# A fused hybrid layer on one Trainium2 core: the first two feed-forward units read the residual times the norm's weight, and the token factor goes onto their result tiles

## The chip, the cores and the metric

The kernel runs on one core of a Trainium2 chip. The metric is the device time of one execution in microseconds (us), as a median over runs.

## What is computed

Two blocks run one after the other on 512 tokens of width 1024, all in float32. The first mixes an RWKV-7 branch and a sparse attention branch. The second has three gated branches and then a feed-forward part with a short convolution. The change touches only the passage into that feed-forward part:

```python
def _rmsnorm(x, g):
    xf = x.astype(jnp.float32)
    r = lax.rsqrt(jnp.mean(xf * xf, axis=-1, keepdims=True) + EPS)
    return (xf * r).astype(x.dtype) * g
...
x = x + _mixer(...)                    # ends in merged @ w_o
h = _rmsnorm(x, norm_ffn_g)            # r: one factor per token, g: one weight per channel
u = _causal_dwconv(h @ w_up, conv_ffn_w)      # 3 taps along the tokens, 2 x 2816 channels
gt, up = jnp.split(u, 2, axis=-1)
x = x + (jax.nn.silu(gt) * up) @ w_down
```

Since r belongs to the token alone, (x * r * g) @ w_up equals ((x * g) @ w_up) * r.

## The kernel before, in words

**Layout.** Activations are stored with channels on the 128 partitions and the 512 tokens along the row: a tensor of width 1024 is 8 chunks of 128x512. Every product of two float32 numbers on TensorE is made from three passes over parts (`tile`, L402 to L404): high x high, low x high, high x low. So every operand is split into a rounded high part and a low part that holds the rest.

**Units.** All weights arrive in a fixed order in units of 8x128 rows by 256 columns (1 MB, `weight_units`). A unit gives two result tiles of 128x512, m = 0 and 1, each with 8 chunks k and three passes: 48 matmuls per unit. There are two weight buffers, taken in turn. For each unit u SyncE loads `w_raw` (`load`), ScalarE copies it into `w_hi` (`split_hi`, L1256), GpSimd takes the difference into `w_lo` (`split_lo`, L1204), and TensorE waits for both (`next_unit`). ScalarE may write the buffer of u only when TensorE is through with u-2 (`slot_used`). ScalarE does so where its own written order has a call of `after_unit()`, which splits the unit two ahead. Whatever stands in front of that call on ScalarE also delays the weights.

**Order within a unit.** `unit_tiles` without `ready` makes tile 0 and then tile 1. With `ready` it goes by chunks, both tiles for each chunk, and waits ahead of each chunk. Result tiles go round 8 PSUM banks in turn; a bank is used again when VectorE has counted it free.

**The passage.** Units "wo2" 0 to 3 (merged @ w_o) are added to the residual `x_res` by VectorE (`residual`, L2196), and ScalarE squares the new chunks (`sq_f`, L1670). VectorE adds the squares of chunks 0 to 5 together (`sum_squares`, L2208). TensorE then sums over the channels (`token_sums`, L384: 12 float32 matmuls of one column each, 24 records), VectorE makes the variance and its reciprocal (L2217, L2220), ScalarE the root (L1267), and TensorE spreads the 512 token factors over all partitions (`spread`, L393: 4 matmuls, 8 records). Only then does VectorE scale each chunk by weight and token factor (`scaled_chunk`, L1747), ScalarE rounds it (`hi_chunks`, L1302) and VectorE takes the low part (`lo_chunk`, L1758); unit "up" 0 starts on chunk 0 as soon as that is there.

**The up units.** There are 22 (`FC`). For unit i and each tile m, ScalarE writes the last convolution tap from the bank to `conv_f` (L1678), VectorE adds the two other taps from the bank (L2459) and frees the bank. ScalarE then calls `after_unit()` and makes the sigmoid (L1682); VectorE multiplies twice (L2465, L2467) and splits the result in parts for the down product (L1736, L1737), which counts `act_ready`. `conv_f` has two sets, so the taps of unit i wait until unit i-2 has counted `act_ready`. Every one of the three engines follows its own written order.

Of the kernel before, what the change touches and what calls it, by code (L numbers as in the profile page):

```python
# [16 lines left out]
F32 = mybir.dt.float32  # L17
F32R = mybir.dt.float32r
ALU = mybir.AluOpType
# [101 lines left out]
MASS_ORDER = [(odd, q) for q in range(NT) for odd in range(2)]  # L121
SCORE_AT = [(0, 0), (0, P), (1, 0), (2, 0)]
FIRST_POOL_UNIT = 9
MIX_ORDER = [*range(NI, CH), *range(NI)]


# [4 lines left out]
def build(nc, dram, out):  # L131
# [3 lines left out]
    with ctx:  # L135
        base = -(-nc.sbuf_base // 32) * 32

        def at(name, offset, shape, dt=F32):
            return nc.alloc_sbuf_tensor_at(name, [P] + shape, dt, offset=base + offset)
# [3 lines left out]
        def sem(name):  # L143
            if name not in sems:
                sems[name] = ctx.enter_context(nc.semaphore(name))
            return sems[name]
# [96 lines left out]
        merged_hi = at("merged_hi", R0 + 32768, [CH, T], F32R)  # L243
        merged_lo = at("merged_lo", R0 + 49152, [CH, T], F32R)
        sq_f = at("sq_f", R0, [CH, T])
        pad_a = at("pad_a", R0 + 73728, [KA - 1 + T])
        rs_mix = tmp[2][:, 0:T]
        u_sig = tmp[2][:, 0:T]
# [48 lines left out]
        def take(eng, key):  # L297

            b, n = seq[key]
            eng.wait_ge(full[b], n + 1)  # L300
            return ps[b]
# [5 lines left out]
        def evacuated(eng, key):  # L307

            b, n = seq[key]
            eng.wait_ge(free[b], n + 1)  # L310
# [24 lines left out]
        def _(pe):  # L335
# [39 lines left out]
            def token_sums(key, sq):  # L375

                b = bank(key)
                for n, c in enumerate((0, CH - 2, CH - 1)):
                    if n:
                        pe.wait_ge(sem("sq_" + key), c + 1)  # L380
                    else:
                        pe.wait_ge(sem("summed_" + key), 1)
                    for t in range(NT):
                        mm = nc.tensor.matmul(b[:, t:t + 1], sq[:, c, t * P:t * P + P], ones[:, 0:1], start=n == 0 and t == 0,  # L384
                                              stop=n == 2, skip_group_check=True)
                done(mm, key)

            def spread(key, col, b=None):

                if b is None:  # L390
                    b = bank(key)
                for t in range(NT):
                    mm = nc.tensor.matmul(b[:, t * P:t * P + P], col[:, t:t + 1].to_broadcast([P, P]), ident[:, :], start=True, stop=True)  # L393
                done(mm, key)
# [16 lines left out]
            def unit_tiles(what, i, xh, xl, width=T, tiles=2, ready=None, branch=None, order=range(CH), between=None):  # L411

                u = next_unit(what)
                keys = [(what, i, m) if branch is None else (what, branch, i, m) for m in range(tiles)]
                if ready is None:
                    for m in range(tiles):
                        b = bank(keys[m])
                        done(tile(b, u, m * P, width, xh, xl), keys[m])
                        if m == 0 and between is not None:
                            between()  # L420
                else:
                    bs = [bank(key) for key in keys]
                    for n, k in enumerate(order):
                        if callable(ready):
                            ready(k)
                        else:
                            pe.wait_ge(sem(ready), n + 1)
                        for m in range(tiles):
                            mm = tile(bs[m], u, m * P, width, xh, xl, start=n == 0, stop=n == CH - 1, ks=[k])
                            if n == CH - 1:  # L430
                                done(mm, keys[m])
                unit_last[u] = keys[-1]
# [641 lines left out]
            gated(1)  # L1074
            for i in range(4):
                unit_tiles("wo2", i, merged_hi, plain(merged_lo), ready=None if i else "merged_ready")
            token_sums("f", sq_f)
            pe.wait_ge(sem("tok_f_ready"), 1)
            spread("rs_f", tok_rs)
            for i in range(FC):  # L1080
                unit_tiles("up", i, oh, ol, ready=None if i else "ffn_ready")
            for i in range(4):
                bs = None
                for k0 in (0, 8, 16):
# [157 lines left out]
        def _(act):  # L1242
# [17 lines left out]
            def root(t=rs[:, :], done="rs_ready"):  # L1260

                if done == "rs_ready":
                    roots[0] += 1
                    act.wait_ge(sem("var_ready"), roots[0])
                else:
                    act.wait_ge(sem(done.replace("ready", "var")), 1)
                A(t, t, ACT.Sqrt).then_inc(sem(done), 1)  # L1267
# [30 lines left out]
            def hi_chunks(which, name):  # L1298

                for c in range(*which):  # L1300
                    act.wait_ge(sem(name + "_scaled"), c + 1)
                    A(op_hi[:, c, :], tmp[c % 2][:, 0:T], ACT.Copy).then_inc(sem(name + "_hi"), 1)  # L1302
# [228 lines left out]
            def after_unit():  # L1531

                nonlocal u
                split_hi(u + 2)
                u += 1
# [127 lines left out]
            for i in range(4):  # L1663
                filled(act, ("wo2", i, 1))
                after_unit()
                if i == 2:
                    A(misc[:, 127:128], ones[:, 0:1], ACT.Sqrt)
                for c in (2 * i, 2 * i + 1):
                    evacuated(act, ("wo2", i, c % 2))
                    A(sq_f[:, c, :], x_res[:, c, :], ACT.Square).then_inc(sem("sq_f"), 1)  # L1670
            root(tok_rs, "tok_f_ready")
            hi_chunks((0, CH), "ffn")
            for i in range(FC):
                for m in range(2):
                    if i >= 2:
                        act.wait_ge(sem("act_ready"), i - 1)

                    A(conv_f[i % 2][m][:, 0:T], take(act, ("up", i, m))[:, :], ACT.Copy,  # L1678
                      scale=pcol("conv_ffn_w_2", 4 * FC + FC * m + i)).then_inc(sem("tap_ready"), 1)
                after_unit()  # L1680
                evacuated(act, ("up", i, 0))
                A(sig_f[i % 2][:, 0:T], conv_f[i % 2][0][:, 0:T], ACT.Sigmoid).then_inc(sem("cg_sig"), 1)  # L1682
            for i in range(4):
# [14 lines left out]
        def _(dve):  # L1698
# [504 lines left out]
            def sum_squares(key, sq, i):  # L2203

                dve.wait_ge(sem("sq_" + key), 2 * i + 2)
                for c in (2 * i, 2 * i + 1):
                    if c:
                        ins = V.tensor_tensor(sq[:, 0, :], sq[:, 0, :], sq[:, c, :], ALU.add)  # L2208
                        if c == CH - 3:
                            ins.then_inc(sem("summed_" + key), 1)  # L2210
                        else:
                            link(ins)
# [220 lines left out]
            for c in range(CH):  # L2433
                parts(conv_b[:, c, :], op2_hi[:, c, :], op2_lo[:, c, :], "op2_ready1")
            gate_steps(1)
            for i in range(4):
                if i:
                    sum_squares("f", sq_f, i - 1)
                residual("wo2", i)
            for i in range(4):  # L2440
                for m in range(2):
                    evacuated(dve, ("wo2", i, m))
            token_variance("f", 1.0 / D, EPS2).then_inc(sem("tok_f_var"), 1)
            r_f = take(dve, "rs_f")
            for c in range(CH):
                scaled_chunk("norm_ffn_g_2", c, r_f, "ffn")
                if c:
                    lo_chunk(c - 1, "ffn")
# [4 lines left out]
            for i in range(FC):  # L2453
                for m in range(2):
                    b, y = take(dve, ("up", i, m)), conv_f[i % 2][m]
                    dve.wait_ge(sem("tap_ready"), 2 * i + m + 1)
                    for back in (1, 2):
                        w = pcol("conv_ffn_w_2", 2 * FC * (2 - back) + FC * m + i)
                        ins = V.scalar_tensor_tensor(y[:, back:T], b[:, 0:T - back], w, y[:, back:T], ALU.mult, ALU.add)  # L2459
                        if back == 1:  # L2460
                            link(ins)
                    evac(ins, ("up", i, m))
                g, y = sig_f[i % 2][:, 0:T], conv_f[i % 2]
                dve.wait_ge(sem("cg_sig"), i + 1)
                link(V.tensor_tensor(g, g, y[0][:, 0:T], ALU.mult))  # L2465
                evacuated(dve, ("up", i, 1))
                link(V.tensor_tensor(g, g, y[1][:, 0:T], ALU.mult))  # L2467
                lo = act_lo[:, i, :] if i < 16 else act_lo2[:, i - 16, :]
                parts(g, act_hi[:, i, :], lo, "act_ready")
# [73 lines left out]
```

## Time and profile before

| what | value |
|---|---|
| median of 3 runs | 1470.88 us (1470.73 to 1476.52) |
| the profiled execution, its own time | 1469.24 us |
| its span in the trace | 1467.4 us (1.84 us lie around it) |
| mean granted TensorE clock | 0.982 |
| TensorE matmuls busy | 1408.8 us, 96% of the span |
| VectorE, ScalarE, GpSimd busy | 64%, 33%, 33% |
| DMA | 125.14 MB, mean 85 GB/s |

A time in the trace is counted from the start of the span. "PE" is TensorE, "PEld" its weight loads, "DVE" VectorE, "ACT" ScalarE, "POOL" GpSimd. `L402` is a line of the kernel. A matmul of 512 columns is shown with its full length of about 0.39 us, while the next starts 0.23 us after it, so the distance between starts is what counts. "<-" in brackets names what an engine was waiting for. The granted clock is 1.00 at 2.4 GHz and 0.50 at 1.2 GHz.

### The profile page before, as it was taken

The page shows a single profiled execution, that of the slowest core. Times are in us where ns is not written, and L with a number is a line of the kernel's source. Part 1 is how long each engine was busy: PE and PEld are TensorE (multiplying, and loading weights), DVE is VectorE, ACT ScalarE, POOL GpSimd, SP SyncE. Part 2 cuts the span into 40 slices and gives each one's busy share as a digit, 9 for nine tenths or more (in the row PEclk, how much of TensorE's full clock was granted, in tenths as well). Part 3 has the DMA queues.
Part 4 walks back from the last instruction along what each step waited for, and adds up shares of the span by engine and source line. Part 5 has one row for each costly group of instructions (what it writes and reads, how often), then busy time and mean ns, then how long its engine had stood idle before and what let it go on. Part 6 is the DMA issues. An engine that isn't in the chain of part 4 may idle for free.

```text
span 1467.4 us, 18610 instructions
## 1 busy us (share of the span) xinstructions
PE 1408.8 (96%) x7612; PEld 1144.1 (78%) x7612; DVE 933.8 (64%) x1322; ACT 487.7 (33%) x663; POOL 487.6 (33%) x131
## 2 busy tenths in 40 slices
PE   7999978699998999999999999999989999999997
PEld 6778646587888877888888887878878888888886
DVE  6679868735413357769969974762457888885122
ACT  5443367243324232122222223322233333332121
POOL 0004110012535323343434433334423443443441
PEclk9999999799999999999999999999989999999999
DMA  6221000023314211232232231222222223222221
GB/s 206 87 87 58 29 2 2 4 85 118 129 71 144 87 58 58 86 100 102 86 105 97 87 115 58 86 98 104 86 87 86 87 88 113 87 99 95 84 96 58
DMA packets 21349, 125.14 MB, mean 85 GB/s; under 512 B 2384, under 2 KB 3408, under 8 KB 7696
## 3 DMA queue, kind: packets, MB, share of 16 engines
q1 hardware_dynamic: 20752, 121.71, 23.6%
q10 hardware_dynamic: 512, 2.23, 0.4%
q8 instruction: 61, 1.00, 0.3%
q14 instruction: 24, 0.20, 0.0%
HBM read 121.84 MB, written 2.10 MB: 84 GB/s over the span
## 4 chain that ended last, share of the span: by engine, by line
PE 88%; DVE 8%; ACT 3%; issue 1%; DMA 0%; DVEq 0%; SPq 0%; ACTq 0%
PE bank L402 25%; PE bank L404 24%; PE bank L403 24%; PE bank L1008 1%; PE bank L1024 1%; PE bank L354 1%; DVE conv_b L2406 1%; PE bank L393 1%; ACT prob L1409 1%; PE bank L877 1%; PE bank L958 1%; PE bank L626 0%; ACT probT L1415 0%; PE bank L362 0%; DVE op_hi L1736 0%
## 5 line engine op out<-in xcount | busy, mean ns | idle before, releaser
L1204 POOL TENSOR_TENSOR w_lo<-w_raw,w_hi 128x2048 fp32r<-128x2048 f32 (+1 forms) x102 | 468.2, 4590 | 762.8 <-ACT w_hi L1256 746.9
L402 PE MATMUL bank<-op_hi,w_hi 128*128 128x512 f32 x1344 | 529.8, 394 | 6.4 <-DVE op_lo L1758 2.3
L404 PE MATMUL bank<-op_hi,w_lo 128*128 128x512 f32 x1344 | 525.9, 391 | 0.0
L403 PE MATMUL bank<-op_lo,w_hi 128*128 128x512 f32 x1344 | 525.9, 391 | 0.0
L402 PEld LDWEIGHTS bank<-op_hi,w_hi 128*128 128x128 f32 x1344 | 253.6, 189 | 63.7 <-issue 6.3
L404 PEld LDWEIGHTS bank<-op_hi,w_lo 128*128 128x128 f32 x1344 | 253.3, 188 | 54.6
L403 PEld LDWEIGHTS bank<-op_lo,w_hi 128*128 128x128 f32 x1344 | 253.4, 189 | 54.0 <-issue 0.7
L1256 ACT ACTIVATE w_hi<-w_raw 128x2048 fp32r<-128x2048 f32 (+2 forms) x109 | 205.6, 1887 | 265.3 <-PE bank L404 265.3
L2299 DVE SCALAR_TENSOR_TENSOR bank<-pad_b,par,bank 128x512 f32<-128x512 f32 x232 | 175.3, 756 | 7.8
L2465 DVE TENSOR_TENSOR tmp<-tmp,conv_f 128x512 f32<-128x512 f32 x22 | 101.6, 4617 | 16.4 <-ACT tmp L1682 16.4
L2196 DVE TENSOR_TENSOR x_res<-bank,x_res 128x512 f32<-128x512 f32 x24 | 16.5, 691 | 136.9 <-PE bank L404 136.8
L402 PE MATMUL bank<-act_hi,w_hi 128*128 128x512 f32 x176 | 69.4, 394 | 0.0
L404 PE MATMUL bank<-act_hi,w_lo 128*128 128x512 f32 x176 | 69.3, 394 | 0.0
L403 PE MATMUL bank<-act_lo,w_hi 128*128 128x512 f32 x176 | 69.2, 393 | 0.0
L1678 ACT ACTIVATE conv_f<-bank,par 128x512 f32<-128x512 f32 x33 | 22.7, 689 | 101.6 <-PE bank L404 101.6
L2459 DVE SCALAR_TENSOR_TENSOR conv_f<-bank,par,conv_f 128x511 f32<-128x511 f32 x66 | 49.2, 747 | 10.9 <-ACT conv_f L1678 9.7
L2380 DVE TENSOR_TENSOR tmp<-bank,gate 128x512 f32<-128x512 f32 x16 | 11.1, 692 | 57.8 <-PE bank L404 57.7
L1605 ACT ACTIVATE gate<-bank,par 128x512 f32<-128x512 f32 x24 | 16.4, 688 | 79.6 <-PE bank L404 79.6
L404 PEld LDWEIGHTS bank<-act_hi,w_lo 128*128 128x128 f32 x176 | 33.1, 188 | 7.8
L403 PEld LDWEIGHTS bank<-act_lo,w_hi 128*128 128x128 f32 x176 | 33.1, 188 | 7.7
L402 PEld LDWEIGHTS bank<-act_hi,w_hi 128*128 128x128 f32 x176 | 33.1, 188 | 7.6
L1195 POOL TENSOR_SCALAR_AFFINE_SELECT score<-score 128x128 f32<-128x128 f32 x3 | 0.9, 295 | 90.7 <-DVE misc L1896 90.7
(374 smaller groups left out, 1702.0 us busy)
## 6 DMA issues: line engine op xcount, KB each, us to landing
w_raw<-in_w_units SPq DMA_DIRECT2D x104, 1024.0 KB, 4.9
w_raw<-in_w_units SPq DMA_DIRECT2D x4, 768.0 KB, 4.2
x_res<-in_x SPq DMA_DIRECT2D x8, 256.0 KB, 6.5
x_res<-in_x ACTq DMA_DIRECT2D x2, 1024.0 KB, 6.3
out<-x_res SPq DMA_DIRECT2D x8, 256.0 KB, 2.2
w_raw<-in_w_units SPq DMA_DIRECT2D x3, 512.0 KB, 9.0
w_raw<-in_w_units SPq DMA_DIRECT2D x4, 256.0 KB, 5.6
mem_tok<-in_mem SPq DMA_DIRECT2D x1, 1024.0 KB, 5.2
```

What stands on the lines that cost most here:

```text
L354: mm = nc.tensor.transpose(b[:, j * P:j * P + rows], src, ident[0:rows, 0:rows])
L402: nc.tensor.matmul(b[:, 0:width], h, xh[:, x0 + k, 0:width], start=start and k == ks[0], stop=False)
L403: nc.tensor.matmul(b[:, 0:width], h, xl(x0 + k, width), start=False, stop=False)
L404: mm = nc.tensor.matmul(b[:, 0:width], l, xh[:, x0 + k, 0:width], start=False, stop=stop and k == ks[-1])
L1204: nc.gpsimd.tensor_tensor(w_lo[u % 2][:, 0:nk, :], w_raw[u % 2][:, 0:nk, :], w_hi[u % 2][:, 0:nk, :].bitcast(F32), ALU.subtract).then_inc( ...
L1256: A(w_hi[u % 2][:, 0:nk, 0:n], w_raw[u % 2][:, 0:nk, 0:n], ACT.Copy).then_inc(hi_ready, 1)
L1605: evac(A(gates[m][:, :], take(act, ("pg", branch, i, m))[:, :], ACT.Sigmoid, bias=pcol("b_gate_2", 8 * branch + 2 * i + m)), ("pg", branch ...
L1678: A(conv_f[i % 2][m][:, 0:T], take(act, ("up", i, m))[:, :], ACT.Copy, scale=pcol("conv_ffn_w_2", 4 * FC + FC * m + i)).then_inc(sem("tap_ ...
L2196: evac(V.tensor_tensor(x, b[:, :], x, ALU.add), (what, i, m))
L2299: ins = V.scalar_tensor_tensor(to, pad[:, k:k + T], pcol("conv_b_w_2", 8 * k + i), y, ALU.mult, ALU.add)
L2459: ins = V.scalar_tensor_tensor(y[:, back:T], b[:, 0:T - back], w, y[:, back:T], ALU.mult, ALU.add)
L2465: link(V.tensor_tensor(g, g, y[0][:, 0:T], ALU.mult))
```

## The change

Three things are changed. VectorE and ScalarE make, for each residual chunk, the parts of x times the norm's weight (`plain_hi`, `plain_lo`), beside the squares. Units "up" 0 and 1 read these parts, with the token sums placed ahead of chunk 3 of unit 0 and the spread ahead of chunk 7; VectorE multiplies each of their four result tiles by the token factor, in the bank, before the taps. And ScalarE splits the weights of "up" 2 ahead of `hi_chunks` and those of "up" 3 behind it, both ahead of the taps of unit 0; the calls behind the taps stay from unit 2 on. From unit 2 on the normed parts are read as before, with the waits for their chunks in unit 2.

```diff
--- before.py
+++ after.py
@@ -121,6 +121,7 @@
 MASS_ORDER = [(odd, q) for q in range(NT) for odd in range(2)]
 SCORE_AT = [(0, 0), (0, P), (1, 0), (2, 0)]
 FIRST_POOL_UNIT = 9
+PLAIN_UNITS = 2
 MIX_ORDER = [*range(NI, CH), *range(NI)]
 
 
@@ -243,6 +244,8 @@
         merged_hi = at("merged_hi", R0 + 32768, [CH, T], F32R)
         merged_lo = at("merged_lo", R0 + 49152, [CH, T], F32R)
         sq_f = at("sq_f", R0, [CH, T])
+        plain_hi = at("plain_hi", R0 + 16384, [CH, T], F32R)
+        plain_lo = at("plain_lo", 65536, [CH, T], F32R)
         pad_a = at("pad_a", R0 + 73728, [KA - 1 + T])
         rs_mix = tmp[2][:, 0:T]
         u_sig = tmp[2][:, 0:T]
@@ -1074,11 +1077,20 @@
             gated(1)
             for i in range(4):
                 unit_tiles("wo2", i, merged_hi, plain(merged_lo), ready=None if i else "merged_ready")
-            token_sums("f", sq_f)
-            pe.wait_ge(sem("tok_f_ready"), 1)
-            spread("rs_f", tok_rs)
-            for i in range(FC):
-                unit_tiles("up", i, oh, ol, ready=None if i else "ffn_ready")
+
+            def statistics(k):
+                pe.wait_ge(sem("plain_ready"), k + 1)
+                if k == 3:
+                    token_sums("f", sq_f)
+                elif k == CH - 1:
+                    pe.wait_ge(sem("tok_f_ready"), 1)
+                    spread("rs_f", tok_rs)
+
+            unit_tiles("up", 0, plain_hi, plain(plain_lo), ready=statistics)
+            for i in range(1, PLAIN_UNITS):
+                unit_tiles("up", i, plain_hi, plain(plain_lo))
+            for i in range(PLAIN_UNITS, FC):
+                unit_tiles("up", i, oh, ol, ready=None if i > PLAIN_UNITS else "ffn_ready")
             for i in range(4):
                 bs = None
                 for k0 in (0, 8, 16):
@@ -1667,17 +1679,24 @@
                     A(misc[:, 127:128], ones[:, 0:1], ACT.Sqrt)
                 for c in (2 * i, 2 * i + 1):
                     evacuated(act, ("wo2", i, c % 2))
+                    A(plain_hi[:, c, :], x_res[:, c, :], ACT.Copy, scale=pcol("norm_ffn_g_2", c)).then_inc(sem("plain_hi"), 1)
                     A(sq_f[:, c, :], x_res[:, c, :], ACT.Square).then_inc(sem("sq_f"), 1)
             root(tok_rs, "tok_f_ready")
+            after_unit()
             hi_chunks((0, CH), "ffn")
+            for i in range(1, PLAIN_UNITS):
+                after_unit()
             for i in range(FC):
                 for m in range(2):
                     if i >= 2:
                         act.wait_ge(sem("act_ready"), i - 1)
+                    if i < PLAIN_UNITS:
+                        act.wait_ge(sem("up_scaled"), 2 * i + m + 1)
 
                     A(conv_f[i % 2][m][:, 0:T], take(act, ("up", i, m))[:, :], ACT.Copy,
                       scale=pcol("conv_ffn_w_2", 4 * FC + FC * m + i)).then_inc(sem("tap_ready"), 1)
-                after_unit()
+                if i >= PLAIN_UNITS:
+                    after_unit()
                 evacuated(act, ("up", i, 0))
                 A(sig_f[i % 2][:, 0:T], conv_f[i % 2][0][:, 0:T], ACT.Sigmoid).then_inc(sem("cg_sig"), 1)
             for i in range(4):
@@ -2433,15 +2452,24 @@
             for c in range(CH):
                 parts(conv_b[:, c, :], op2_hi[:, c, :], op2_lo[:, c, :], "op2_ready1")
             gate_steps(1)
+            def plain_parts(i):
+                for c in (2 * i, 2 * i + 1):
+                    dve.wait_ge(sem("plain_hi"), c + 1)
+                    V.scalar_tensor_tensor(plain_lo[:, c, :], x_res[:, c, :], pcol("norm_ffn_g_2", c), plain_hi[:, c, :].bitcast(F32),
+                                           ALU.mult, ALU.subtract).then_inc(sem("plain_ready"), 1)
+
             for i in range(4):
                 if i:
                     sum_squares("f", sq_f, i - 1)
+                    plain_parts(i - 1)
                 residual("wo2", i)
+            plain_parts(3)
             for i in range(4):
                 for m in range(2):
                     evacuated(dve, ("wo2", i, m))
             token_variance("f", 1.0 / D, EPS2).then_inc(sem("tok_f_var"), 1)
             r_f = take(dve, "rs_f")
+            link(V.tensor_copy(rs[:, :], r_f[:, :]))
             for c in range(CH):
                 scaled_chunk("norm_ffn_g_2", c, r_f, "ffn")
                 if c:
@@ -2453,6 +2481,8 @@
             for i in range(FC):
                 for m in range(2):
                     b, y = take(dve, ("up", i, m)), conv_f[i % 2][m]
+                    if i < PLAIN_UNITS:
+                        V.tensor_tensor(b[:, :], b[:, :], rs[:, :], ALU.mult).then_inc(sem("up_scaled"), 1)
                     dve.wait_ge(sem("tap_ready"), 2 * i + m + 1)
                     for back in (1, 2):
                         w = pcol("conv_ffn_w_2", 2 * FC * (2 - back) + FC * m + i)
```

## Rows read from the trace of the kernel before

**Rows 1.** page, part 1: engine, busy us (share), instructions
```profile
PE 1408.8 (96%) x7612; PEld 1144.1 (78%) x7612; DVE 933.8 (64%) x1322; ACT 487.7 (33%) x663; POOL 487.6 (33%) x131
```

**Rows 2.** page, part 4: the chain that ended last
```profile
PE 88%; DVE 8%; ACT 3%; issue 1%; DMA 0%; DVEq 0%; SPq 0%; ACTq 0%
```

**Rows 3.** timeline of TensorE, 1074 to 1100 us: start, length, instruction, idle before
```profile
1080.48 0.95 PE L384 MATMUL bank<-ones,sq_f 128*128 128x1 f32 x8
1083.24 2.44 PE L384 MATMUL bank<-ones,sq_f 128*128 128x1 f32 x16 [1.82 <-ACT sq_f L1670]
1086.49 2.08 PE L393 MATMUL bank<-ident,misc 128*128 128x128 f32 x8 [0.81 <-ACT misc L1267]
1090.89 0.77 PE L402 MATMUL bank<-op_hi,w_hi 128*128 128x512 f32 x1 [2.32 <-DVE op_lo L1758]
...
1094.44 0.56 PE L404 MATMUL bank<-op_hi,w_lo 128*128 128x512 f32 x1
```

**Rows 4.** timeline of ScalarE, 1032 to 1140 us
```profile
1047.16 1.92 ACT L1256 ACTIVATE w_hi<-w_raw 128x2048 fp32r<-128x2048 f32 x1 [9.28 <-PE bank L404]
...
1058.36 1.92 ACT L1256 ACTIVATE w_hi<-w_raw 128x2048 fp32r<-128x2048 f32 x1 [8.24 <-PE bank L404]
...
1080.76 1.91 ACT L1256 ACTIVATE w_hi<-w_raw 128x2048 fp32r<-128x2048 f32 x1 [6.72 <-PE bank L404]
1082.58 1.13 ACT L1670 ACTIVATE sq_f<-x_res 128x512 f32<-128x512 f32 x2
1086.23 0.21 ACT L1267 ACTIVATE misc<-misc 128x4 f32<-128x4 f32 x1 [2.52 <-DVE misc L2220]
...
1098.48 0.63 ACT L1302 ACTIVATE op_hi<-tmp 128x512 fp32r<-128x512 f32 x1 [0.75 <-DVE tmp L1747]
...
1106.41 1.28 ACT L1682 ACT_TABLE_LOAD   x1
...
1126.30 1.91 ACT L1256 ACTIVATE w_hi<-w_raw 128x2048 fp32r<-128x2048 f32 x1
...
1137.18 1.91 ACT L1256 ACTIVATE w_hi<-w_raw 128x2048 fp32r<-128x2048 f32 x1
```

**Rows 5.** timeline of VectorE, 1032 to 1102 us
```profile
1050.15 4.17 DVE L2208 TENSOR_TENSOR sq_f<-sq_f 128x512 f32<-128x512 f32 x1 [2.38 <-ACT sq_f L1670]
...
1090.05 0.69 DVE L1758 TENSOR_TENSOR op_lo<-tmp,op_hi 128x512 fp32r<-128x512 f32 x1
...
1099.57 0.69 DVE L1758 TENSOR_TENSOR op_lo<-tmp,op_hi 128x512 fp32r<-128x512 f32 x1 [0.52 <-ACT op_hi L1302]
```

**Rows 6.** timeline of GpSimd, 1032 to 1140 us
```profile
1049.16 4.62 POOL L1204 TENSOR_TENSOR w_lo<-w_raw,w_hi 128x2048 fp32r<-128x2048 f32 x1 [6.12 <-ACT w_hi L1256]
...
1082.75 4.50 POOL L1204 TENSOR_TENSOR w_lo<-w_raw,w_hi 128x2048 fp32r<-128x2048 f32 x1 [6.57 <-ACT w_hi L1256]
```

**Rows 7.** lines by shape on VectorE, 500 to 1467 us: count, busy us, mean ns
```profile
L2465 DVE TENSOR_TENSOR tmp<-tmp,conv_f 128x512 f32<-128x512 f32 x22 | 101.6, 4617 | 16.4 <-ACT tmp L1682 16.4
...
L2459 DVE SCALAR_TENSOR_TENSOR conv_f<-bank,par,conv_f 128x511 f32<-128x511 f32 x33 | 24.6, 746 | 9.7 <-ACT conv_f L1678 9.7
...
L2196 DVE TENSOR_TENSOR x_res<-bank,x_res 128x512 f32<-128x512 f32 x16 | 11.1, 691 | 102.9 <-PE bank L404 102.9
```

**Rows 8.** timeline of TensorE, 1452 to 1467 us
```profile
1454.52 2.88 PE L384 MATMUL bank<-ones,sq 128*128 128x1 f32 x24
1458.20 2.05 PE L393 MATMUL bank<-ident,misc 128*128 128x128 f32 x16 [0.81 <-ACT misc L1267]
```

**Rows 9.** windows, TensorE: stretch, length, busy (records), granted clock, DMA share, GB/s
```profile
145.00:146.00 1.00, 1.00 (x11) 0.93 0.00 0
...
152.00:153.00 1.00, 1.00 (x5) 0.66 0.00 0
...
1463.00:1464.00 1.00, 0.00 (x0) 0.70 1.01 373
```

**Rows 10.** timeline of TensorE, 138 to 154 us
```profile
143.21 4.41 PE L553 MATMUL bank<-pair_ones,kk_sq 128*128 128x2 f32 x32
```


## The prediction

> **What bounds the kernel now.** I read the engine shares first: TensorE is busy for 96% of the span [rows 1], and the chain that ended last lies on it for 88% [rows 2]. So a change is worth what it takes out of TensorE's stream, and nothing else. Then I read TensorE's timeline at the passage [rows 3]. The last matmul of "wo2" leaves the array free at 1080.48. Sums, a wait of 1.82, more sums, a wait of 0.81, the spread and a wait of 2.32 follow, and "up" 0 starts at 1090.89. Its first nine matmuls take 3.94 us (1090.89 to 1094.44 + 0.39), where nine at the usual distance take 2.05: the granted clock had fallen. The usual distance comes from ScalarE's timeline: its weight splits follow each other at 10.88 us in the up units [rows 4], which is one unit, 0.227 a matmul. So "up" 1 starts at 1094.83 + 39 x 0.227 = 1103.7, and 23.2 us lie between the end of "wo2" and it, for 10.9 us of work. "Up" 4 starts at 1103.7 + 3 x 10.9 = 1136.4. That is the time to compare with.
>
> **What must stay on TensorE.** The sums without a wait take 2.88 us, and 16 records of the spread take 2.05, so the 8 here 1.0 [rows 8]. Unit 0 now runs from 1080.5: chunks 0 to 2 (18 matmuls) 4.1 to 1084.6, sums to 1087.5, chunks 3 to 6 5.5 to 1093.0, spread to 1094.0, chunk 7 to 1095.4. "Up" 1 ends at 1106.3 and "up" 2 would end at 1117.2. If nothing else waits, the gain is 23.2 - 14.9 = 8.3 us. That is the ceiling, 0.56%.
>
> **What is added ahead of it, at nothing.** ScalarE makes eight rounded copies, 0.57 each by its squares [rows 4]. They stand behind the weight split of the same step, so no weights are late; for the last two chunks the squares are done at 1082.6 + 4 x 0.57 = 1084.9, and the sums need the last one at about 1086.5. VectorE makes eight low parts of 0.75. Six of them stand beside "wo2", where the adding of squares leaves it free; the tile behind them is late by 1.5 us at most, and it still comes before the second tile of its unit. The seventh meets GpSimd's split, which lasts to 1087.25 [rows 6], so the last low part may come at 1088.6, against a need at 1091.6 and 1094.0. Behind them in VectorE's order stands the variance: it is done at 1089.0, the root at 1089.3 (0.2 us, rows 4), against a need at 1093.0. Cover gone, each of these would cost its own lateness, and there are 3 us of it.
>
> **What moves on ScalarE, GpSimd and VectorE.** The split of "up" 2's weights now stands ahead of the eight rounding copies. It can begin when unit 0 is through, at 1095.5, and ends at 1097.4; GpSimd's part runs 1097.5 to 1102.1 (4.62, rows 6). VectorE's low part of chunk 0 becomes ready at 1098.0, in the middle of that. What this costs is read from a like pair: an addition with both inputs in SBUF started at 1050.15 while GpSimd had been splitting since 1049.16, took 4.17 us instead of 0.69 and ended 0.54 after it [rows 5, 6]. All 22 products of the up units average 4617 ns for the same cause, while operations with an input in PSUM keep 691 and 746 ns [rows 7]. The trace of before has no low part of this line beside a GpSimd split, so it lies between 0.7 (no block) and the end of the split plus 0.54. I take the block, since the nearest rows all show it: low part 0 ends at 1102.65. From low part 0 to low part 7 it took 9.5 us [rows 5], so the last one ends at 1112.2, and ScalarE's last copy about 1.15 ahead, at 1111.0 [rows 4]. The Trainium skill (SBUF — State Buffer, "Who interferes with whom") has this as a rule: a VectorE instruction with two SBUF inputs and a GpSimd instruction that reads SBUF exclude each other for a whole instruction. It says of this line what no row of it shows; if the rule did not hold here, the time would be the first rival's.
>
> Only now does ScalarE split "up" 3: 1111.0 to 1112.9, GpSimd 1113.0 to 1117.6. "Up" 3 starts at 1117.7 instead of 1117.2, a wait of 0.5, and ends at 1128.6. VectorE starts unit 0 at 1112.2 (before: 1104.0), and each tile of units 0 and 1 is a chain: factor 0.69, ScalarE's tap 0.69, two taps 1.53, with the handovers 2.95. The factor and the copy of it to SBUF read PSUM, so they are priced as the residual's 0.69 [rows 7]; no row shows the factor itself, and 0.5 to 0.9 moves the end by less than 1 us. Unit 0's tiles end at 1118.1, the sigmoid with its table load of 1.28 at 1118.4 [rows 4], two products and two parts at 1121.0. Unit 1's tiles run to 1126.9; its second ScalarE tap is done at 1125.35, its sigmoid at 1126.0. **Here is the step that decides.** The weights of "up" 4 are split behind the taps of unit 2, and these stand behind the sigmoid of unit 1: taps 1127.2, split 1129.1, GpSimd 1129.2 to 1133.8. "Up" 3 is through at 1128.6, so TensorE waits 5.3 us and starts "up" 4 at 1133.9, 2.5 us ahead of before. After that it doesn't recur: "up" 5's weights are due at 1144.8 and there at about 1139.6, and VectorE, at 9.6 us of work a unit against 10.9, catches up. The banks hold: "up" 3 takes those of unit 0, freed at 1115.1 and 1118.1, needed at 1117.7 and 1123.1. SyncE's loads need only the two splits of the unit two before and come 6 us or more ahead.
>
> **The clock.** After the last spread TensorE stands still from 1460.25, and the clock fell at 1463.4 (0.70 of the window, rows 8, 9). So in a wait of 5.3 us I expect it to fall, and to cost what it costs now behind the passage, 1.9 us (3.94 - 2.05). The other row for it: 12 matmuls at half rate after 147.5, 2.4 us; the bounds are 0 and 3.2 (16 matmuls). The Trainium skill (TensorE: Matmul & The Clock Gate, Part 1) gives two rates, chosen by how busy the engine has been of late; the rows agree in that.
>
> **The pitch.** "wo2", whose operands lie elsewhere, takes 11.20 a unit, the up units 10.88 [rows 4]. The new operands of units 0 and 1 may cost 0 or 2 x 0.3; one of the two is ahead of the chain that decides, so I take 0.3.
>
> **Sum.** 2.5 - 1.9 - 0.3 = 0.3 us gained. The profiled execution had 1469.24 (span 1467.4 and 1.84 around it), so 1468.9. The median of the runs is 1.64 higher; on that footing the forecast is 1470.6. A difference under 0.5% (7.35 us) is about what a measurement of this kernel can't tell from none.
>
> **Rivals.** (a) *The block does not come, or ScalarE is earlier.* Low part 0 ends at 1098.7, the whole chain is 3.9 us earlier, "up" 4 starts at 1130.0 after a wait of 1.9, for which I add no fall of the clock: 2.5 + 3.9 - 0.3 = 6.1 gained, 1464.8. Against it: all 22 products. For it: no row of this line. (b) *No wait at all.* 8.3, less 0 to 0.6 for the pitch, 1462.6 to 1463.2. That needs "up" 4's weights 5.3 us earlier, against ScalarE's written order. (c) *The narrow sums lower the clock inside unit 0.* At 143.21 a dense block of 32 such records stood between wide matmuls, for 4.41 us; the clock fell inside the block, at 145.9 (0.93 of the window from 145), and came back only at 152.7 [rows 9, 10]. Here 24 records of the kind last 2.88. If the clock falls on them too, some 12 matmuls run at half rate, 2.4 us, and since the end of unit 0 starts the deciding chain, all of it arrives: 0.3 - 2.4 = -2.1, slower, 1473.0. Against it: the same 24 records at 1454.52, with the spread behind them, left the clock at full until 1463. (d) *The change doesn't do what it says*, for instance the plain parts come late and unit 0 waits for them as before: 1470.9.
>
> **Chances.** Forecast 0.52 (1469 to 1472, by the bounds of the clock and the pitch), (a) 0.20, (b) 0.09, (c) 0.14, (d) 0.05. The range takes in the forecast, (a) and (c): 1464.5 to 1473.5. Faster by over 0.5% needs (b), 0.09. Slower by over 0.5% needs 7 us more than the sum has, which only (c) with a second long wait could give: 0.04. The rest, 0.87, is within.
>
> **What would show it.** Right: "up" 0 starts at 1080.5; VectorE's first low part of L1758 lasts over 4 us; TensorE waits about 0.5 ahead of "up" 3 and about 5 ahead of "up" 4, for GpSimd's `w_lo`, and the clock dips there; "up" 4 starts near 1134. Wrong: no wait ahead of "up" 4, or waits ahead of later units too, or a dip of the clock at 1087.

## The result, and the profile after

The changed kernel took 1474.84 us as the median of 20 runs (1471.94 to 1481.42) against 1470.75 for the kernel before in the same rounds; the ratio is 1.0024, 95% interval 1.0014 to 1.0034. It is slower by about 3.5 us, outside the stated range. The profiled execution took 1475.07 us, with a span of 1473.2.

The page has little of it: TensorE's busy time is up by 2.6 us, the span by 5.8. First the engine line of part 1, to be read against [rows 1]:

```profile
PE 1411.4 (96%) x7612; PEld 1145.5 (78%) x7612; DVE 939.8 (64%) x1335; ACT 492.6 (33%) x671; POOL 487.6 (33%) x131
```

The waits of TensorE in the changed kernel from 1040 to 1200 us (engine, line, what it waited for, total us, times, longest) say where to look. The three waits of the passage in [rows 3] are gone, and one of 8.8 is there that wasn't:

```profile
PE bank L405 <- DVE conv_f L2489: 8.8, 1, 8.8
```

Its place is in TensorE's timeline (start, length, instruction). These lines answer to [rows 3]:

```profile
1085.24 2.73 PE L387 MATMUL bank<-ones,sq_f 128*128 128x1 f32 x24
...
1095.00 1.05 PE L396 MATMUL bank<-ident,misc 128*128 128x128 f32 x8
...
1108.03 0.40 PE L407 MATMUL bank<-plain_hi,w_lo 128*128 128x512 f32 x1
1117.26 0.76 PE L405 MATMUL bank<-op_hi,w_hi 128*128 128x512 f32 x1 [8.84 <-DVE conv_f L2489]
...
1122.09 0.63 PE L407 MATMUL bank<-op_hi,w_lo 128*128 128x512 f32 x1
1122.52 0.45 PE L405 MATMUL bank<-op_hi,w_hi 128*128 128x512 f32 x1
```

Sums and spread stand inside unit 0 with no wait, as the change meant. Unit 1 is through at 1108.3. Then "up" 2 stands still until 1117.26, and it is released by line 2489, VectorE's tap on a result tile of unit 0. The tap frees a PSUM bank. Twelve matmuls at 0.43 follow, as the clock had fallen. The windows show it twice (stretch, length, TensorE busy and records, granted clock, DMA share, GB/s):

```profile
1084.00:1088.00 4.00, 4.00 (x32) 1.00 0.00 0
1088.00:1089.00 1.00, 1.00 (x4) 0.75 0.22 25
1089.00:1091.00 2.00, 2.00 (x6) 0.50 0.81 266
1091.00:1092.00 1.00, 1.00 (x4) 0.54 1.00 426
1092.00:1096.00 4.00, 4.00 (x23) 1.00 0.05 18
...
1112.00:1113.00 1.00, 0.00 (x0) 0.70 0.00 0
1113.00:1122.00 9.00, 4.74 (x11) 0.50 0.14 35
```

The first fall is inside unit 0, right behind the block of narrow sums (rival c); the second is inside the new wait. VectorE's timeline answers to [rows 5]:

```profile
1083.95 5.21 DVE L2458 SCALAR_TENSOR_TENSOR plain_lo<-x_res,par,plain_hi 128x512 fp32r<-128x512 f32 x2 [1.95 <-ACT plain_hi L1682]
...
1100.00 4.69 DVE L1777 TENSOR_TENSOR op_lo<-tmp,op_hi 128x512 fp32r<-128x512 f32 x1 [1.77 <-ACT op_hi L1314]
...
1113.16 0.69 DVE L1777 TENSOR_TENSOR op_lo<-tmp,op_hi 128x512 fp32r<-128x512 f32 x1 [0.17 <-ACT op_hi L1314]
1114.00 0.70 DVE L2485 TENSOR_TENSOR bank<-bank,rs 128x512 f32<-128x512 f32 x1
1115.47 1.53 DVE L2489 SCALAR_TENSOR_TENSOR conv_f<-bank,par,conv_f 128x511 f32<-128x511 f32 x2 [0.77 <-ACT conv_f L1696]
```

Low part 0 is blocked for 4.69 us as forecast, the last low part ends at 1113.85, and the first tile of unit 0 is done with at 1117.0. That is the moment for which "up" 2 waits. GpSimd's splits of "up" 2 and "up" 3, of the kind of [rows 6], are these:

```profile
1099.52 4.62 POOL L1216 TENSOR_TENSOR w_lo<-w_raw,w_hi 128x2048 fp32r<-128x2048 f32 x1 [11.58 <-ACT w_hi L1268]
1114.94 4.54 POOL L1216 TENSOR_TENSOR w_lo<-w_raw,w_hi 128x2048 fp32r<-128x2048 f32 x1 [10.79 <-ACT w_hi L1268]
```

**One count for all kernels.** The time ahead of the passage differs between executions by several us, as the clock stays low for longer or shorter in its first 500 us (the mark below stands between 1035.2 and 1044.7). So I compare the profiled executions from one instruction that all have, GpSimd's split that begins in the first "wo2" unit, to the end of the span. In the timeline of GpSimd the kernel before has

```profile
1037.96 5.08 POOL L1204 TENSOR_TENSOR w_lo<-w_raw,w_hi 128x2048 fp32r<-128x2048 f32 x1 [6.02 <-ACT w_hi L1256]
```

and the changed kernel

```profile
1038.59 5.07 POOL L1216 TENSOR_TENSOR w_lo<-w_raw,w_hi 128x2048 fp32r<-128x2048 f32 x1 [6.03 <-ACT w_hi L1268]
```

That is 1467.4 - 1038.0 = 429.4 and 1473.2 - 1038.6 = 434.6, so 5.2 us of the 5.8 come from the passage on. (The expectations below call it the fourth "wo2" unit before the passage, counting back; it is "wo2" 0.) Starts of units are counted from the same mark.

**Where the 5.2 us are.** "Up" 2 starts 78.7 after that mark; before it started at 1103.7 + 10.9 - 1038.0 = 76.6, so 2.1 later. Its first thirteen matmuls take 5.55 us (1117.26 to 1122.81), 2.6 more than at 0.227 each, so "up" 3 starts 4.7 later than before (92.2 against 87.5). The last spread of the kernel happened to run largely at half rate, 3.39 us against 2.05 [rows 8], and the final scaling began 1.72 after its start in place of 1.19, 0.5:

```profile
1463.51 3.39 PE L396 MATMUL bank<-ident,misc 128*128 128x128 f32 x16 [0.81 <-ACT misc L1279]
```

Together 5.2.

### The profile page after: what moved, and what is told of

Same layout as the page of the kernel before. It is cut to its first block, busy times and chain, and to the rows that moved or that the text cites. A ratio compares the mean times of both kernels' runs of the same rounds, so it can differ in the third digit from the quotient of the medians.

```text
span 1473.2 us, 18632 instructions
## 1 busy us (share of the span) xinstructions
PE 1411.4 (96%) x7612; PEld 1145.5 (78%) x7612; DVE 939.8 (64%) x1335; ACT 492.6 (33%) x671; POOL 487.6 (33%) x131
## 4 chain that ended last, share of the span: by engine, by line
PE 87%; DVE 8%; ACT 3%; issue 1%; DMA 0%; DVEq 0%; SPq 0%; ACTq 0%
PE bank L405 24%; PE bank L406 24%; PE bank L407 24%; PE bank L1011 1%; PE bank L1027 1%; PE bank L357 1%; DVE conv_b L2425 1%; ACT prob L1421 1%; PE bank L396 1%; DVE op_lo L1777 1%; PE bank L880 1%; PE bank L961 1%; ACT w_hi L1268 1%; PE bank L629 0%; ACT probT L1427 0%
## 5 line engine op out<-in xcount | busy, mean ns | idle before, releaser
L405 PE MATMUL bank<-op_hi,w_hi 128*128 128x512 f32 x1312 | 517.8, 395 | 13.0 <-DVE conv_f L2489 8.8
L407 PE MATMUL bank<-op_hi,w_lo 128*128 128x512 f32 x1312 | 513.8, 392 | 0.0
L406 PE MATMUL bank<-op_lo,w_hi 128*128 128x512 f32 x1312 | 513.8, 392 | 0.0
L405 PEld LDWEIGHTS bank<-op_hi,w_hi 128*128 128x128 f32 x1312 | 247.7, 189 | 69.4 <-issue 13.0
L407 PEld LDWEIGHTS bank<-op_hi,w_lo 128*128 128x128 f32 x1312 | 247.5, 189 | 53.3
L406 PEld LDWEIGHTS bank<-op_lo,w_hi 128*128 128x128 f32 x1312 | 247.7, 189 | 52.8 <-issue 0.7
L2495 DVE TENSOR_TENSOR tmp<-tmp,conv_f 128x512 f32<-128x512 f32 x22 | 95.0, 4318 | 14.0 <-ACT tmp L1701 14.0
```

Source lines behind the costliest of these rows:

```text
L405: nc.tensor.matmul(b[:, 0:width], h, xh[:, x0 + k, 0:width], start=start and k == ks[0], stop=False)
L406: nc.tensor.matmul(b[:, 0:width], h, xl(x0 + k, width), start=False, stop=False)
L407: mm = nc.tensor.matmul(b[:, 0:width], l, xh[:, x0 + k, 0:width], start=False, stop=stop and k == ks[-1])
```

## The experiments

After the trace I had one theory with a second bound behind it. *Banks*: the rotation has seven banks, not eight, and a unit in the waiting form asks for both its banks at its start, so "up" 2 needs the bank of unit 0's first tile. *Weights*: what I had forecast as deciding, the late split of "up" 4's weights, is the true bound, and the bank wait only stands in front of it. All counts stand in one table at the end of this part.

### The eighth bank

```diff
+            rest = [ring[(turn[0] + j) % len(ring)] for j in range(len(ring))]
+            ring[:] = [CONV_BANK] + rest
+            turn[0] = 0
             unit_tiles("up", 0, plain_hi, plain(plain_lo), ready=statistics)
```

The bank that held the long convolution (taken out of the rotation at line 947 of the kernel before, idle since the last tap) goes back in. VectorE's own first wait on that bank, for the long convolution, keeps its old count.

> The changed kernel, with the bank that served the long convolution put back into TensorE's rotation just ahead of up 0: eight banks instead of seven. Bank theory: the 8.8 us wait ahead of up 2 is for the bank that up 0's first tile holds until VectorE has scaled it and added its taps (1117.0), because up 2 asks for both its banks at its start. With eight it asks for other banks: no wait ahead of up 2, which starts at about 1107. Then the weights decide as forecast: a wait of 1 to 2 us ahead of up 3, one of about 5 us ahead of up 4, up 4 starts at about 1135.5 instead of 1141.8, and with a fall of the clock there the kernel is within 2 us of the kernel before (ratio 0.999 to 1.001). Rival (the order of the weights alone sets the loss, the bank wait only stands in front of it): up 4 starts no earlier than 1140 and the ratio stays near 1.0024.

Measured: 1472.37 us, ratio 0.9986 (0.9975 to 0.9998), count 430.2. TensorE's timeline has two waits left among the up units:

```profile
1119.76 0.47 PE L406 MATMUL bank<-op_hi,w_hi 128*128 128x512 f32 x1 [0.34 <-issue]
...
1135.80 0.77 PE L406 MATMUL bank<-op_hi,w_hi 128*128 128x512 f32 x1 [4.90 <-issue]
```

They are ahead of "up" 3 and "up" 4. In ScalarE's timeline the split of "up" 4 stands where the forecast put it, behind unit 1's sigmoid and unit 2's two taps, and GpSimd's half (from 1130.80, 4.90 long) ends 0.1 ahead of the release:

```profile
1127.14 0.62 ACT L1706 ACTIVATE tmp<-conv_f 128x512 f32<-128x512 f32 x1
1127.66 1.26 ACT L1701 ACTIVATE conv_f<-bank,par 128x512 f32<-128x512 f32 x2
1128.80 1.92 ACT L1273 ACTIVATE w_hi<-w_raw 128x2048 fp32r<-128x2048 f32 x1
```

So with eight banks the forecast's own picture comes out: waits of 0.34 and 4.90 against 0.5 and 5.3, and a time within 0.3% of before. (For this run I had expected 1 to 2 us ahead of "up" 3.) "Up" 4 starts 97.1 behind the mark, 1.3 ahead of the kernel before (98.4) where the forecast had 2.5; what is missing is the fall of the clock in unit 0 (1.6, see below), less 0.4 for the shorter wait.

### The second bank asked for late

```diff
-                unit_tiles("up", i, oh, ol, ready=... "ffn_ready")
+                    for m in range(2):
+                        bm = bank(("up", i, m))
+                        for k in range(CH):
+                            if m == 0:
+                                pe.wait_ge(sem("ffn_ready"), k + 1)
+                            mm = tile(bm, u, m * P, T, oh, ol, start=k == 0, stop=k == CH - 1, ks=[k])
+                        done(mm, ("up", i, m))
```

> The changed kernel with seven banks, where up 2 is worked tile by tile, so that it asks for its second bank only behind its first tile. Bank theory: up 2 starts at about 1107, its second tile waits at about 1112.6 for the bank that is freed at 1117.0, 4 to 4.5 us instead of 8.8, and about 2 us are left of the wait for up 4's weights; 3 to 6 us faster than the changed kernel, ratio to the kernel before 0.998 to 1.001. Rival (weights alone): no gain over the changed kernel, 1.0024.

Measured: 1472.48 us, ratio 0.9990 (0.9977 to 1.0003), count 430.0. Its timeline:

```profile
1114.57 0.50 PE L405 MATMUL bank<-op_hi,w_hi 128*128 128x512 f32 x1 [2.19 <-DVE conv_f L2500]
...
1133.27 0.47 PE L405 MATMUL bank<-op_hi,w_hi 128*128 128x512 f32 x1 [2.08 <-issue]
```

The wait for VectorE's tap has moved from the start of "up" 2 to its second tile. It is 2.2 and not 4 to 4.5, for two reasons. "Up" 2 starts 69.7 behind the mark, 1.3 us later than the 1107 of my expectation (1107 - 1038.6 = 68.4), which is what the fall of the clock in unit 0 has taken. And a tile alone uses up a chunk in 0.69 us while VectorE makes one in 1.39, so the first tile waits for chunks and ends 1.1 us later. With seven banks still, 4.6 of the 5.2 us are back (0.5 of them at the last spread, which here ran at full rate, 2.05 us). It was the bank, and the moment at which it is asked for.

### The weights alone, and both

```diff
             for i in range(FC):
+                if i == 1:
+                    after_unit()
...
-                if i >= PLAIN_UNITS:
+                if i > PLAIN_UNITS:
                     after_unit()
```

> The changed kernel with the split of up 4's weights moved from behind the taps of unit 2 to ahead of the taps of unit 1, nothing else. Bank theory: the wait ahead of up 2 is untouched, and behind it the weights of up 4 weren't late in the changed kernel, so nothing is gained: 1.0024 (1.0015 to 1.0035). Weights theory (the step I had named as the deciding one): 2 us or more gained.

Measured: 1474.39 us, ratio 1.0019 (1.0002 to 1.0037), count 434.7. The wait ahead of "up" 2 is unchanged, and no wait for weights stood behind it in the changed kernel (GpSimd's split of "up" 4 ended at 1138.2, and the unit started at 1141.6). With seven banks the weights are no bound.

```profile
1113.85 0.77 PE L405 MATMUL bank<-op_hi,w_hi 128*128 128x512 f32 x1 [8.83 <-DVE conv_f L2491]
```

> Both edits: eight banks, and up 4's weights split ahead of the taps of unit 1. Bank theory with the weights as the second bound: neither the wait ahead of up 2 nor that ahead of up 4, only 1 to 2 us ahead of up 3; up 4 starts at about 1130.5, 6 to 7 us ahead of the kernel before, ratio about 0.9955 (0.994 to 0.997). If the eighth bank alone (the first run) already gave this, the weights never counted.

Measured: 1472.19 us, ratio 0.9995 (0.9978 to 1.0011), count 428.9. A miss: I expected 0.9955. The wait ahead of "up" 4 is gone, and one ahead of "up" 5 has come:

```profile
1151.68 0.56 PE L406 MATMUL bank<-op_hi,w_hi 128*128 128x512 f32 x1 [3.83 <-issue]
```

Why is in the timelines of GpSimd and VectorE. The earlier split falls on the low part of unit 0's product, which has both inputs in SBUF, and VectorE loses 4.4 us with it:

```profile
1128.33 4.59 POOL L1221 TENSOR_TENSOR w_lo<-w_raw,w_hi 128x2048 fp32r<-128x2048 f32 x1 [2.61 <-ACT w_hi L1273]
```

```profile
1128.39 5.08 DVE L1763 TENSOR_TENSOR act_lo<-tmp,act_hi 128x512 fp32r<-128x512 f32 x1
```

Everything behind that on VectorE is later, with it the taps of unit 3 on ScalarE, and behind those stands the split of "up" 5.

### Both splits early, and the sums in three parts

The first of these also moves the split of "up" 5 ahead of the taps of unit 2 (`if i in (1, 2)` above, `if i > PLAIN_UNITS + 1` below). The second adds:

```diff
-                if k == 3:
-                    token_sums("f", sq_f)
+                if 2 <= k < 5:
+                    n, c = k - 2, (0, CH - 2, CH - 1)[k - 2]
...
+                    for t in range(NT):
+                        mm = nc.tensor.matmul(sums[0][:, t:t + 1], sq_f[:, c, t * P:t * P + P], ones[:, 0:1], ...)
```

> The changed kernel with eight banks, up 4's weights split ahead of the taps of unit 1 and up 5's ahead of the taps of unit 2. Counted from GpSimd's split of the fourth wo2 unit before the passage to the end of the span the kernel before has 429.5 us, the changed kernel 434.6, and the version with only up 4's split early 428.9, with 3.8 us of waiting ahead of up 5. Theory (the wait goes to the next unit whose split stands behind VectorE's backlog, and up 5 is the last such one): no wait over 0.5 us ahead of any up unit, and with the fall of the clock gone too 423 to 424 us, ratio 0.995 to 0.997. Rival (the backlog passes the wait on to up 6 and further): again 3 us or more of waiting, 428 to 430 us.

Measured: 1469.82 us, ratio 0.9986 (0.9970 to 1.0002), count 428.6. The rival was right: the wait had passed on to "up" 6, 2.65 us, whose split stands behind the taps of unit 4:

```profile
1154.84 0.47 PE L406 MATMUL bank<-op_hi,w_hi 128*128 128x512 f32 x1 [2.65 <-issue]
```

> As e5_both_splits_early, with the twelve narrow matmuls of the token sums given out in three fours, ahead of chunks 2, 3 and 4 of unit 0, in place of one block. If the block of narrow matmuls is what lowered the clock for 4 us inside unit 0 (granted 0.50 from about 1088.7 to 1092), the clock stays at 1.00 there and 1.5 to 2 us more are gained, 421 to 422.5 us by the same count, ratio 0.994 to 0.996. If something else lowers it, nothing changes.

Measured: 1467.55 us, ratio 0.9966 (0.9952 to 0.9980), count 426.0, so 2.6 less than without it. The 421 to 422.5 expected had counted on no wait ahead of "up" 6 either. Over windows of 1 us in the up units and the passage the clock was low for 3.4 us in place of 6.8; the 3.4 that are left begin in the wait ahead of "up" 6. The wait ahead of "up" 6 is the same (2.70). In TensorE's timeline and its window the narrow matmuls now stand in three eights of records, and the clock stays up:

```profile
1082.98 0.95 PE L1094 MATMUL bank<-ones,sq_f 128*128 128x1 f32 x8
1085.24 0.95 PE L1094 MATMUL bank<-ones,sq_f 128*128 128x1 f32 x8
1087.51 0.95 PE L1094 MATMUL bank<-ones,sq_f 128*128 128x1 f32 x8
```

```profile
1082.00:1092.00 10.00, 10.00 (x57) 1.00 0.31 106
```

> The changed kernel (seven banks, splits where the change puts them), with only the token sums given out in three fours. Clock theory: unit 0 ends 1.5 to 2 us earlier, the chain through ScalarE, the blocked low part and VectorE's first tile that ends the wait for the bank starts from there, so the whole gain arrives: 432.5 to 433.2 us by the count above, ratio 1.001 to 1.002. The 8.8 us wait stays.

Measured: 1474.43 us, ratio 1.0011 (0.9996 to 1.0026), count 432.6, so 2.0 less than the changed kernel, with the wait of 8.84 as it was. The starts of the units say what the dense block costs, and the two pairs agree: 1.6 us. "Up" 1 starts 57.1 behind the mark in place of 58.7 in both pairs, "up" 2 here 77.1 in place of 78.7, "up" 3 there 79.5 in place of 81.1. The rest of the 2.0 and 2.6 lies at other falls of the clock: here 0.9 less behind the wait of 8.84 and 0.5 more at the last spread, there 0.9 less at the last spread. (The interval of the ratio alone wouldn't tell this one from the changed kernel.)

### The control

> The kernel before, with the eighth bank put back at the same place, nothing else. Bank theory: there VectorE keeps up with TensorE and no unit waits for a bank, so nothing changes: 429 to 430 us by the same count, ratio 0.999 to 1.001. If the eighth bank gains by itself here, the gain of e1_eighth_bank says nothing of the change.

Measured: 1471.75 us, ratio 0.9999 (0.9984 to 1.0015). No gain by itself. The count of this one profiled execution is 432.0, 2.5 above the kernel before, which I hadn't expected. No wait is longer. The clock stayed low for longer at the old passage, in its windows

```profile
1086.00:1099.00 13.00, 9.87 (x32) 0.50 0.23 81
```

where the kernel before had nine such microseconds:

```profile
1085.00:1094.00 9.00, 5.88 (x19) 0.50 0.35 117
```

Of the 2.5 us, 0.6 lie in the sums and 1.0 in the first matmuls of "up" 0; the last spread, 3.46 us in place of 2.05, has the remaining 0.9. The edit adds no work to any of these. So single counts can differ by 2.5 us by how the clock falls alone. The 4.4 and more that hang on the bank are above that; what is smaller is read here from waits and from the starts of units.

### All splits ahead of the taps

```diff
             for i in range(FC):
+                if 1 <= i < FC - 1:
+                    after_unit()
...
-                if i >= PLAIN_UNITS:
-                    after_unit()
```

With eight banks and the scattered sums.

> As e6_sums_scattered, but the weights of every up unit from 4 on and of the first down units are split ahead of the taps of the unit three before, never behind taps. Theory (what waits is always the first split that stands behind VectorE's backlog in ScalarE's order; here none does): no wait of 0.5 us or more ahead of any up unit, the clock at 1.00 through all of them, and by the count from GpSimd's split of the fourth wo2 unit before the passage to the end 421 to 422 us, where e6_sums_scattered has 426.0 and the kernel before 429.4; ratio 0.9935 to 0.9955. Rival (VectorE, held one unit behind, becomes the bound, or holds banks too long): a wait ahead of a later up unit, or ahead of the last down weights, and 424 us or more.

Measured: 1463.11 us, ratio 0.9938 (0.9916 to 0.9960), count 422.5, half a microsecond above the 421 to 422 expected. TensorE's waits from 1030 to 1450 us are one line, and the clock is at 1.00 in every window from 1080 to 1170:

```profile
PE bank L406 <- issue: 0.3, 1, 0.3
```

This version beats both kernels, by 9 us against the kernel before (6 to 12 by the interval); the counts of the two profiled executions differ by 6.9.

> As e8_all_splits_ahead, with the eighth bank taken out of the rotation again: the sums scattered and all splits ahead of the taps, seven banks. Bank theory: the bank is a bound of its own, so the wait of 8.8 us ahead of up 2 and the fall of the clock behind it are back, and nothing of the order of the weights helps: 432 to 433.5 us by the count (the changed kernel with scattered sums had 432.6, e8_all_splits_ahead 422.5), ratio 1.000 to 1.003. Rival (the order of the splits was the main thing and the bank a side effect): under 427 us.

Measured: 1473.39 us, ratio 1.0012 (0.9992 to 1.0031), count 432.3. With the one bank out of the rotation again, 9.8 us of the count are back:

```profile
1119.49 0.77 PE L405 MATMUL bank<-op_hi,w_hi 128*128 128x512 f32 x1 [8.80 <-DVE conv_f L2501]
```

| kernel | waits ahead of up units, us | count, us | ratio to before |
|---|---|---|---|
| before | 2.32 (up 0), with 1.82 and 0.81 in the passage | 429.4 | |
| changed | 8.84 (up 2) | 434.6 | 1.0024 |
| eighth bank | 0.34 (up 3), 4.90 (up 4) | 430.2 | 0.9986 |
| second bank asked late | 2.19 (up 2, tile 1), 2.08 (up 4) | 430.0 | 0.9990 |
| up 4's split early, seven banks | 8.83 (up 2) | 434.7 | 1.0019 |
| the same, eight banks | 0.33 (up 3), 3.83 (up 5) | 428.9 | 0.9995 |
| up 4's and 5's split early, eight | 0.34 (up 3), 2.65 (up 6) | 428.6 | 0.9986 |
| the same, sums scattered | 0.33 (up 3), 2.70 (up 6) | 426.0 | 0.9966 |
| changed, sums scattered | 8.84 (up 2) | 432.6 | 1.0011 |
| before, eighth bank | 2.32 (up 0) | 432.0 | 0.9999 |
| all splits ahead, sums scattered, eight | 0.32 (up 3) | 422.5 | 0.9938 |
| the same, seven banks | 8.80 (up 2) | 432.3 | 1.0012 |

## Why the prediction was wrong

**The step that failed** is one sentence: "The banks hold: 'up' 3 takes those of unit 0, freed at 1115.1 and 1118.1, needed at 1117.7 and 1123.1." It counts eight banks, as the layout section does ("Result tiles go round 8 PSUM banks in turn"). At the passage the rotation has seven: line 947 has taken one out. From "up" 0 on, the takers are two tiles, the sums, the spread, two tiles of "up" 1 and the first tile of "up" 2, which makes seven; so "up" 2's second tile, not "up" 3's first, comes round to unit 0's first bank. And since "up" 2 is in the waiting form it asks for both banks at its start. The time at which that bank is freed was right in the forecast (1115.1; measured 1117.0, of which 0.6 is the later start of the passage and 1.3 to 1.4 the clock in unit 0). The need for it was put at 1117.7 and is at 1108.3. VectorE's lag itself was in the forecast (1112.2 for its start on unit 0's tiles), but not what it means for the banks: in the kernel before that start is at 1104.0, 10.6 us ahead of the start of "up" 2, and in the changed kernel at 1114.0, 5.7 us behind the moment at which "up" 2 could have started. The line of the kernel before is

```profile
1104.01 2.97 DVE L2459 SCALAR_TENSOR_TENSOR conv_f<-bank,par,conv_f 128x511 f32<-128x511 f32 x4 [3.75 <-ACT conv_f L1678]
```

Of the 8.84 us of waiting, 4.0 are the block of low part 0 (4.69 in place of 0.69). That is an estimate, the length of this low part less that of the others; no run took the block away.

**What came out right.** TensorE's start on unit 0 with no wait for the plain parts; the blocked low part (4.69 us, and 4.545 for one low part of the plain ones); the factor on the bank at 0.69 to 0.70; the handover of 2.9 a tile (1114.00 to 1116.92). The ceiling of 8.3 us is nearly reached: in the version without any other wait, "up" 8 starts 134.0 behind the mark against 141.9 before, 7.9 sooner, and 0.3 of the rest is the wait ahead of "up" 3. (Its count gains 0.9 less, since its last spread ran at half rate, 3.55 us against 2.05.) The deciding step of the forecast, the split of "up" 4 behind unit 2's taps, is there in the version with eight banks to within 0.4 us. In the changed kernel the bank wait hides it: "up" 2 and 3 come so late that the weights don't matter.

**Terms off in size.** What a fall of the clock behind a wait costs isn't one number. Behind the same wait of 8.8 us it was 1.5, 1.7, 2.6 and 2.7 us in four kernels (seven to thirteen slow matmuls); behind the old passage 1.9 and, with the eighth bank, 2.9. Behind the wait of 4.90, the one the forecast had meant, it was 2.0, as priced at 1.9. The bound of 16 matmuls, 3.2 us, comes from no row; the longest fall read here is 14 matmuls. The pitch of the new operands cost 0.1 ("up" 1 takes 10.98 with eight banks), not 0.3. The fall of the clock on the narrow sums, which I had as rival (c) with 0.14 and 2.4 us, does happen, and the sum has no term for it. It costs 1.6 us. Its place was right, its price too high, its chance too low: the counter-evidence was one execution's block at the end of the kernel, which left the clock at full there; inside unit 0 the clock fell in all six profiled versions that have the block there.

**"It doesn't recur" was too simple.** I wrote that after "up" 4 VectorE catches up. With eight banks and the splits as in the change this holds. But moving a split early doesn't remove the wait: in two steps it went from "up" 4 to 5 and to 6. As long as VectorE is behind, whatever split comes next behind taps inherits the lag, and each split that is moved can fall on one more VectorE operation with two SBUF inputs. The wait left only when no split stood behind taps.

**The likely side.** The forecast had the gain eaten by a wait inside the up units plus a fall of the clock, and so close to none. The runs show a loss of that kind, but for another resource and two units earlier, and 3.5 us longer (8.84 against 5.3). That the time still came within 4 to 5 us of the forecast is in part luck: a wait that the forecast didn't see replaced one that it did.

## What to carry to other kernels

When work is taken away from the front of a pipeline, its consumer can fall behind, as VectorE did here. Then count every resource that the consumer gives back, with the true number in the rotation and the place in the code where it is asked for, and not only the ones that waited before. A fixed written order that couples a prefetch to the consumer's progress hands the lag on; put the prefetch ahead of what can lag.

## What the runs showed of the hardware

A dense block of 24 records of one-column float32 matmuls, 2.73 us without a gap between full-width matmuls, was followed by a granted clock of 0.50 for 3.4 us (in the changed kernel from 1088.5 to 1091.9), though the profile shows no idle moment of TensorE there. This is so in all six profiled versions with the block inside unit 0. The same work in three blocks of 0.95 us left the clock at 1.00, in all four that had it so. A burst of DMA falls in the same stretch (share 0.81 to 1.00 from 1089 to 1092), but it isn't the cause: with the sums scattered the share is 0.87 to 0.97 from 1088 to 1091 and the clock stays at 1.00. The Trainium skill (TensorE: Matmul & The Clock Gate, Part 1) describes the half rate as what an idle stretch brings; here it came without one.

At the end of each kernel stands the same block of 2.88 us, then a wait of 0.81 and the last spread. There the clock's fall comes at a different place from one execution to the next: the 16 records of the spread took 2.05 us in four of the twelve profiled executions, the kernel before among them [rows 8], and 2.86 to 3.78 in the other eight.
